# Two of the four channel chunks of a 31-tap depthwise convolution move from vector operations to matrix products with diagonal tap matrices

## The chip, the cores and the metric

One core of a Trainium2 chip runs the whole network. The metric is the device time of one execution in microseconds, the median of several runs. TensorE is called PE below, VectorE DVE, ScalarE ACT, GpSimd POOL and SyncE, which only starts transfers here, SP.

## The reference

The network has ten phases over 256 tokens with 1024 channels in float32: two blocks of a mixer and a convolutional feed-forward, then a second model whose first layer has the *even* mixer. Only that mixer is touched. Cut to what matters:

```python
def even_mixer(h, w_in, w_out, conv_w, conv_b, ln_g, ln_b, q_g, k_g, sinks):
    proj = h @ w_in                                  # 1024 -> 1792 columns
    a_val, a_gate, q, k, v = jnp.split(proj, cuts, axis=-1)
    u = a_val * jax.nn.sigmoid(a_gate)               # 512 channels
    u = lax.conv_general_dilated(u, conv_w[:, None, :], (1,), ((30, 0),),
                                 feature_group_count=512) + conv_b   # 31 taps, causal, per channel
    u = jax.nn.silu(layer_norm(u, ln_g, ln_b))
    q, k = rms_norm_2(q, q_g), rms_norm_2(k, k_g)    # 8 query heads, 2 key heads, 64 wide
    o, _, _ = banded_attention(q, k, v, 127, sinks)
    return jnp.concatenate([u, o], axis=-1) @ w_out
```

## The kernel before, in words

Activations lie transposed: 128 channels of a chunk on the partitions, the 256 tokens in a row. A weight matrix comes in *units* of 128 output columns (512 KB). For each unit SP loads `raw` (a ring of four slots), ACT copies it to a rounded high part `wh` (L507), DVE subtracts to get the low part `wl` (L761), and PE multiplies high by high, high by low and low by high (`tiles`, L1153 to L1155: 24 products of 128 by 128 with 256 tokens) into one of four PSUM banks `gb`. DVE scales the bank into the chunk `y` (L1041). SP's load of unit u+4 waits for DVE's split of unit u, and PE's unit u waits for the chunk that used its bank before.

The even mixer has 14 units on the way in and 8 on the way out. Chunks 0 to 7 of `y` are value and gate of the four channel chunks, chunk 8 is v, 9 is k, 10 to 13 are q. Every engine runs in its own order, and the order of the mixer's own work is one hand-written table `W["even"]` of entries (step, what, number): after unit `step` each engine does its share of the entries of this step, in the order of the table. So one entry places work on several engines at once. The entries that matter are

- `sig` g: ACT turns gate chunk g into its sigmoid, in place (L632).
- `conv` g: DVE does a quarter of the convolution of channel chunk g // 4 (`convolve`, L851 to L869). The first quarter multiplies value and gate into the padded operand `qqf` (L859), writes the first two taps into two accumulators (L861, L862) and adds six taps; the next ones add 8, 8 and 7 taps with one instruction each (L865), and the last adds the two accumulators (L869). There are 16 such entries, the last four between the heads of the attention.
- `turn`: PE transposes v (L1311). `sqr`, `sum`, `norm` g: the norm of q and k for group g (chunks 9 and 10, 11 and 12, 13): POOL squares (L427), PE sums over the head (L1298), ACT takes ln and then exp, each with a table load (L595, L597), DVE multiplies (L818).
- `attn` t: a software pipeline over 8 heads. PE turns the probabilities of head t-3 (L1265), makes the scores of head t (L1254) and the output of head t-4 (L1289); DVE takes the maximum of head t (L911 to L919) and normalises head t-1 (L932 to L946); ACT copies, and exponentiates head t (L544). Every second output DVE writes a low part into `mx` (L977).
- `ln`: the layer norm of the convolved chunks, and the gate (`layer_norm`, L871 to L899, with two PE sums), then the 8 units on the way out (L1166 to L1170).

```python
val, gate = yc(2 * c), yc(2 * c + 1)
for k in range(max(2, 8 * part), min(31, 8 * part + 8)):
    s = (val, gate)[k % 2]
    link_second(nc.vector.scalar_tensor_tensor(out=s, in0=qqf[:, k:k + SEQ], scalar=prm[:, taps + k:taps + k + 1],
                                               in1=s, op0=ALU.mult, op1=ALU.add))
```

Of the kernel before, what the change touches and what calls it, by code (L numbers as in the profile page):

```python
# [11 lines left out]
P = 128  # L12
# [86 lines left out]
def build_program(nc, xin, wa, wb, prm_d, row_d, const_d, bias_d, mask_d, pw_d, out):  # L99
# [21 lines left out]
    with ctx:  # L121
# [37 lines left out]
        qq = sb("qq", [P, 2, 2, SEQ])  # L159
        kk = sb("kk", [P, 2, 2, SEQ])  # L160
# [15 lines left out]
        low = ptb[:, :, :].rearrange("p a (b c) -> p a b c", b=2)  # L176
        ident = con[:, C_ID:C_ID + P]
# [31 lines left out]
        def cross_blocks(b):  # L209
# [16 lines left out]
        NAMES = ("qk_squared qk_sums qk_log qk_rsd qk_normed rotated roped v_transposed v_tokens scores maxima exps "  # L226
                 "probs probs_turned probsT attn_out attn_copied mix_psum mix_sbuf mix_hi mix_lo").split()
        OWN = {"mix1": ("gate_sigs gates_ready k_packed level_scores diag_copied level_copied totals q_up k_up stats "
                        "stats_log stats_rsd c_copied").split(),
               "even": "sigmoids ln_operand ln_sum ln_log ln_rsd ln_out ln_sig".split(), "odd": ["pooled"]}  # L230
# [36 lines left out]
        def row0(hs, t):  # L267
# [17 lines left out]
             "even": [(1, "sig", 0), (2, "conv", 0), (3, "sig", 1), (3, "conv", 1), (4, "conv", 2), (5, "sig", 2), (5, "conv", 3),  # L285
                      (6, "conv", 4), (7, "sig", 3), (7, "conv", 5), (8, "conv", 6), (9, "turn", 0), (9, "conv", 7),
                      (10, "conv", 8), (11, "sqr", 0), (11, "conv", 9), (12, "sum", 0), (12, "norm", 0), (12, "sqr", 1),
                      (12, "conv", 10), (13, "attn", 0), (13, "sum", 1), (13, "norm", 1), (13, "sqr", 2), (13, "conv", 11),
                      (14, "attn", 1), (14, "sum", 2), (14, "norm", 2), (14, "attn", 2), (14, "conv", 12), (14, "attn", 3),
                      (14, "attn", 4), (14, "conv", 13), (14, "attn", 5), (14, "attn", 6), (14, "conv", 14), (14, "attn", 7),  # L290
                      (14, "attn", 8), (14, "conv", 15), (14, "attn", 9), (14, "attn", 10), (14, "attn", 11), (14, "ln", 0)],
# [26 lines left out]
        def bank_of(kind, u):  # L318

            return u % 4 if kind != "mix1" or u < 13 else u % 2  # L320

# [179 lines left out]
        def _(act):  # L501
# [88 lines left out]
            def do(what, g, m, n, kind, l):  # L590
# [39 lines left out]
                elif what == "sig":  # L630
                    act.wait_ge(s_y, Y0[n] + 2 * g + 2)
                    nc.scalar.activation(yc(2 * g + 1), yc(2 * g + 1), ACT.Sigmoid).then_inc(m["sigmoids"], 1)  # L632
                elif what == "ln":
# [109 lines left out]
        def _(dve):  # L743
# [126 lines left out]

            def layer_norm(m):  # L871

                link(nc.vector.tensor_tensor(acc[:, :], yc(0), yc(2), ALU.add))
# [139 lines left out]
            def do(what, g, m, n, kind, l):  # L1013
# [4 lines left out]
                elif what == "gates":  # L1018
                    gates(m, l)
                elif what == "conv":  # L1020
                    convolve(m, g // 4, g % 4)
                elif what == "attn":
                    attention(m, kind, heads(kind), g, l)
                elif what == "level" and 1 <= g <= NL:
                    level(m, g)
                elif what == "post":
                    out_norms(m, l)
                elif what == "ln":
                    layer_norm(m)
                elif what == "pool":  # L1030
                    dve.wait_ge(m["mix_hi"], before(kind, "pool", g) + 1)
                    nc.vector.scalar_tensor_tensor(out=mc(ml, 4 + g), in0=MISC[:, 0:SEQ], scalar=col("ps", g),
                                                   in1=mc(mh, 4 + g).bitcast(f32), op0=ALU.mult, op1=ALU.subtract).then_inc(m["mix_lo"], 1)
# [111 lines left out]
        def _(pe):  # L1145
# [147 lines left out]
            def do(what, g, m, n, kind, l):  # L1293
# [42 lines left out]
                elif what == "post":  # L1336
                    pe.wait_ge(m["mix_sbuf"], 1)
                    pe.wait_ge(s_y, Y0[n] + IN_UNITS[kind])
                    for k, (c, w) in enumerate([(3, 2), (5, 2), (7, 1)]):
# [5 lines left out]
                        last.then_inc(m["mix_psum"], 1)  # L1345
                elif what == "ln":
# [188 lines left out]
```

## Time and profile before

| | us |
|---|---|
| median of 3 runs | 1840.45 |
| the three runs | 1834.74, 1840.45, 1840.59 |
| the profiled execution, its own time | 1835.33 |
| its span | 1833.6 |
| busy in the span: PE, DVE, ACT, POOL | 1673.1, 1273.2, 988.9, 531.1 |
| the even mixer's way in, attention and layer norm (974.6 to 1116.6 us of the span) | 142.0 |

The 1.7 us between the span and the profiled execution's own time lie around the span. Busy times of a stage come from a table of stretches; the granted clock there is a share of full speed, 1.00 being 2.4 GHz and 0.50 being 1.2 GHz. A matmul in f32 appears as two records in the trace, so x4 stands for two products. In a timeline the start of the next row tells more than the duration, since instructions of one engine overlap a little at their ends.

### The profile page before, as it was taken

The numbers are of one execution on the slowest core, as the hardware profiler recorded it, in microseconds if no ns is written. First come the engines' busy times: TensorE is split into PE (matmuls) and PEld (weight loads), VectorE is DVE, ScalarE is ACT, GpSimd is POOL, SyncE is SP. The second block draws the span as 40 slices with busy tenths as digits, with TensorE's granted clock in tenths as the row PEclk, the third lists the DMA queues.
The fourth block names the chain that finished last, engine by engine and source line by source line (L and its number), as shares of the span: only waits on it lengthen the run. The fifth ranks groups of instructions, "written<-read, shape, count | busy, mean of one in ns | idle before, by whom it ended". The sixth has DMA issues, their size and how long they took to land. (4 is left out here: it accounts for less than half of the span.)

```text
span 1833.6 us, 30207 instructions
## 1 busy us (share of the span) xinstructions
PE 1673.1 (91%) x10188; PEld 1448.8 (79%) x10188; DVE 1273.2 (69%) x2018; ACT 988.9 (54%) x1530; POOL 531.1 (29%) x511
## 2 busy tenths in 40 slices
PE   5896899999976999999999476999999999799999
PEld 5785799888856999888888335888888888568888
DVE  5675677756776777667757877777577765757763
ACT  5455466545563666466644344665376535446652
POOL 3040433310312334134410003443144411434430
PEclk9998899999997999999999658999999999789999
DMA  6330355654311456555654202556555654225563
GB/s 229 104 116 24 100 181 185 219 169 139 104 58 57 163 185 204 184 177 188 209 186 133 86 1 86 178 185 215 164 181 185 209 180 149 69 92 184 186 217 102
DMA packets 70793, 274.12 MB, mean 150 GB/s; under 512 B 7872, under 2 KB 9024, under 8 KB 70592
## 3 DMA queue, kind: packets, MB, share of 16 engines
q1 hardware_dynamic: 70272, 271.04, 45.9%
q0 software_dynamic: 448, 2.13, 0.3%
q8 instruction: 43, 0.70, 0.2%
q14 instruction: 30, 0.25, 0.0%
HBM read 272.09 MB, written 1.05 MB: 149 GB/s over the span
## 5 line engine op out<-in xcount | busy, mean ns | idle before, releaser
L761 DVE TENSOR_TENSOR wl<-raw,wh 128x1024 fp32r<-128x1024 f32 (+1 forms) x474 | 626.6, 1322 | 104.7 <-ACT wh L507 98.1
L507 ACT ACTIVATE wh<-raw 128x1024 fp32r<-128x1024 f32 (+1 forms) x474 | 529.2, 1118 | 211.9 <-PE gb L1170 125.2
L1166 PE MATMUL gb<-hx,wh 128*128 128x512 f32 x1540 | 554.0, 399 | 0.0
L1167 PE MATMUL gb<-hx,wl 128*128 128x256 f32 x1540 | 432.3, 281 | 0.0
L1166 PE MATMUL gb<-gux,wh 128*128 128x512 f32 x960 | 341.1, 394 | 0.0
L1166 PEld LDWEIGHTS gb<-hx,wh 128*128 128x128 f32 x1540 | 289.8, 188 | 60.7
L1153 PE MATMUL gb<-hx,wh 128*128 128x256 f32 x1008 | 299.2, 297 | 24.8 <-DVE wl L761 17.4
L1167 PEld LDWEIGHTS gb<-hx,wl 128*128 128x128 f32 x1540 | 291.0, 189 | 7.9
L1154 PE MATMUL gb<-hx,wh 128*128 128x256 f32 x1008 | 288.7, 286 | 0.0
L1155 PE MATMUL gb<-hx,wl 128*128 128x256 f32 x1008 | 288.2, 286 | 0.0
L1167 PE MATMUL gb<-gux,wl 128*128 128x256 f32 x960 | 268.1, 279 | 0.0
L493 POOL TENSOR_TENSOR tap<-tap,rstd 128x256 f32<-128x256 f32 x132 | 175.0, 1326 | 250.9 <-ACT tap L685 141.7
L1153 PEld LDWEIGHTS gb<-hx,wh 128*128 128x128 f32 x1008 | 196.0, 194 | 37.7 <-DVE wl L761 17.0
L1166 PEld LDWEIGHTS gb<-gux,wh 128*128 128x128 f32 x960 | 180.0, 188 | 39.1
L1154 PEld LDWEIGHTS gb<-hx,wh 128*128 128x128 f32 x1008 | 196.2, 195 | 5.2 <-issue 2.9
L496 POOL TENSOR_TENSOR gux<-gu,gux 128x256 f32 x132 | 142.8, 1082 | 197.5 <-ACT gux L694 197.5
L1155 PEld LDWEIGHTS gb<-hx,wl 128*128 128x128 f32 x1008 | 196.0, 194 | 0.0
L1167 PEld LDWEIGHTS gb<-gux,wl 128*128 128x128 f32 x960 | 180.4, 188 | 4.3
L413 POOL TENSOR_TENSOR sq<-x 128x256 f32<-128x256 f32 x70 | 70.0, 1000 | 241.7 <-DVE x L1114 222.2
L524 ACT ACTIVATE hx<-x,prm 128x256 fp32r<-128x256 f32 (+1 forms) x80 | 40.0, 508 | 145.4 <-DVE x L1114 142.9
L1166 PE MATMUL gb<-mx,wh 128*128 128x512 f32 x224 | 86.5, 422 | 12.6 <-DVE mx L899 9.1
L691 ACT ACTIVATE ptb<-gb 128x256 f32<-128x256 f32 x132 | 49.7, 377 | 81.5 <-PE gb L1170 81.5
(213 smaller groups left out, 2140.7 us busy)
## 6 DMA issues: line engine op xcount, KB each, us to landing
raw<-in_wa SPq DMA_DIRECT2D x378, 512.0 KB, 3.5
raw<-in_wb SPq DMA_DIRECT2D x96, 704.0 KB, 4.1
x<-in_x SPq DMA_DIRECT2D x1, 1024.0 KB, 5.0
out_x<-x SPq DMA_DIRECT2D x8, 128.0 KB, 3.2
row<-in_row POOLq DMA_DIRECT2D x1, 836.0 KB, 10.6
tab<-in_bias SPq DMA_DIRECT2D x3, 256.0 KB, 4.6
con<-in_const POOLq DMA_DIRECT2D x1, 544.0 KB, 7.7
tab<-in_bias SPq DMA_DIRECT2D x1, 512.0 KB, 5.2
```

Source lines behind the costliest of these rows:

```text
L413: link(nc.gpsimd.tensor_tensor(sq[:, 0:SEQ], xc, xc, ALU.mult))
L493: nc.gpsimd.tensor_tensor(tap[:, j, :], tap[:, j, :], rstd[:, :], ALU.mult).then_inc(s_up, 1)
L496: nc.gpsimd.tensor_tensor(gul[:, part], gu[:, j, :], guh[:, part].bitcast(f32), ALU.subtract).then_inc(s_gul, 1)
L507: nc.scalar.activation(wh[:, slot, 0:nt * P], raw[:, slot, 0:nt * P], ACT.Copy).then_inc(s_hi, 1)
L524: nc.scalar.activation(hh[:, part], x[:, part], ACT.Copy, scale=prm[:, at0]).then_inc(s_hh, 1)
L691: nc.scalar.activation(low[:, j, 1, :], gb[2 * j + 1][:, SEQ:2 * SEQ], ACT.Copy).then_inc(s_vl, 1)
L761: nc.vector.tensor_tensor(wl[:, slot, 0:nt * P], raw[:, slot, 0:nt * P], wh[:, slot, 0:nt * P].bitcast(f32), ALU.subtract).then_inc(s_lo, 1)
L1153: nc.tensor.matmul(bank, a, rhs_h(k), start=start and k == 0, stop=False)
L1154: nc.tensor.matmul(bank, a, rhs_l(k), start=False, stop=False)
L1155: last = nc.tensor.matmul(bank, b, rhs_h(k), start=False, stop=stop and k == nt - 1)
L1166: nc.tensor.matmul(bank[:, :], a, both(k), start=start and k == 0, stop=False)
L1167: nc.tensor.matmul(bank[:, 0:SEQ], b, high(k), start=False, stop=False)
```

## The change

The channel chunks 0 and 2 stay on DVE (`conv` 0 to 3 and 8 to 11). The chunks 1 and 3 are convolved on PE:

- `operand` (DVE): multiplies value and gate of the chunk into a padded buffer in free chunks of `y`.
- `diag` g (ACT): writes 8 (or 7) diagonal matrices, the identity times the tap of each channel, into a new buffer `dg` of 31 matrices; 62 copies of 128x128 in all. The second chunk's reuse the buffer behind the first's products.
- `taps` g (PE): 8 (or 7) products of a diagonal matrix with the shifted operand, in full f32, summed in PSUM bank `gb[3]`; 62 in all.
- `convolved` (ACT): copies the bank out with the bias.

So the units on the way in have three banks instead of four (`u % 3`). The layer norm waits for both `convolved`. The ln and exp instructions of the norms are as before. Semaphores that a phase doesn't use are no longer made for it.

```diff
+        with ExitStack() as turn:
+            dg = sb("dg", [P, 31, P], f32, turn)
...
+        operand = (y[:, 15 * SEQ:17 * SEQ], y[:, 17 * SEQ:19 * SEQ])
...
-             "even": [(1, "sig", 0), (2, "conv", 0), (3, "sig", 1), (3, "conv", 1), (4, "conv", 2), (5, "sig", 2), (5, "conv", 3),
...
+             "even": [(1, "sig", 0), (1, "diag", 0), (2, "conv", 0), (2, "diag", 1), (3, "sig", 1), (3, "operand", 0),
+                      (3, "conv", 1), (3, "diag", 2), (4, "conv", 2), (4, "diag", 3), (5, "sig", 2), (5, "taps", 0),
+                      (5, "conv", 3), (6, "taps", 1), (6, "conv", 8), (7, "sig", 3), (7, "taps", 2), (7, "operand", 1),
+                      (7, "conv", 9), (8, "taps", 3), (8, "conv", 10), (8, "diag", 4), (9, "turn", 0), (9, "convolved", 0),
+                      (9, "conv", 11), (9, "diag", 5), (10, "diag", 6), (11, "sqr", 0), (11, "diag", 7), (12, "sum", 0),
+                      (12, "norm", 0), (12, "sqr", 1), (12, "taps", 4), (13, "attn", 0), (13, "sum", 1), (13, "norm", 1),
+                      (13, "sqr", 2), (13, "taps", 5), (14, "attn", 1), (14, "sum", 2), (14, "norm", 2), (14, "attn", 2),
+                      (14, "taps", 6), (14, "attn", 3), (14, "attn", 4), (14, "taps", 7), (14, "attn", 5),
+                      (14, "convolved", 1)] + [(14, "attn", t) for t in range(6, 12)] + [(14, "ln", 0)],
...
         def bank_of(kind, u):
 
+            if kind == "even":
+                return u % 3
             return u % 4 if kind != "mix1" or u < 13 else u % 2
...
+                elif what == "diag":
+                    if g >= 4:
+                        act.wait_ge(m["taps_multiplied"], g - 3)
+                    for k in taps_of(g % 4):
+                        last = nc.scalar.activation(dg[:, k, :], ident, ACT.Copy, scale=col("ecw", 31 * (2 * (g // 4) + 1) + k))
+                    last.then_inc(m["diagonals"], 1)
+                elif what == "convolved":
+                    c = 2 * g + 1
+                    act.wait_ge(m["taps_multiplied"], 4 * g + 4)
+                    nc.scalar.activation(yc(2 * c), gb[3][:, 0:SEQ], ACT.Identity, bias=col("ecb", c)).then_inc(m["convolved"], 1)
...
+                dve.wait_ge(m["sigmoids"], c + 1)
+                nc.vector.memset(operand[g][:, 0:30], 0.0)
+                nc.vector.tensor_tensor(operand[g][:, 30:30 + SEQ], yc(2 * c), yc(2 * c + 1), ALU.mult).then_inc(m["operands"], 1)
...
+                elif what == "taps":
+                    c = g // 4
+                    pe.wait_ge(m["operands"], c + 1)
+                    pe.wait_ge(m["diagonals"], g + 1)
+                    if g == 4:
+                        pe.wait_ge(m["convolved"], 1)
+                    for k in taps_of(g % 4):
+                        last = nc.tensor.matmul(gb[3][:, 0:SEQ], dg[:, k, :], operand[c][:, k:k + SEQ], start=k == 0, stop=k == 30)
+                    last.then_inc(m["taps_multiplied"], 1)
```

The order of ACT at the start of the mixer, before (L632 is the sigmoid, L507 the split of a unit):

```order
L530 ACTIVATE rstd<-rstd 128x256
L507 ACTIVATE wh<-raw 128x1024 x2
L632 ACT_TABLE_LOAD
L632 ACTIVATE y<-y 128x256
L507 ACTIVATE wh<-raw 128x1024 x2
```

and with the change (L643 is the sigmoid, L518 the split, L648 a diagonal matrix):

```order
L541 ACTIVATE rstd<-rstd 128x256
L518 ACTIVATE wh<-raw 128x1024 x2
L643 ACT_TABLE_LOAD
L643 ACTIVATE y<-y 128x256
L648 ACTIVATE dg<-con,prm 128x128 x8
L518 ACTIVATE wh<-raw 128x1024
L648 ACTIVATE dg<-con,prm 128x128 x8
L518 ACTIVATE wh<-raw 128x1024
```

Eight diagonal matrices now stand ahead of the split of unit 6, and eight more ahead of that of unit 7.

The order of PE behind the last unit of the way in, before (L1254 scores, L1298 sums of squares, L1265 turned probabilities, L1289 outputs):

```order
L1155 MATMUL gb<-hx,wl 128x256
L1254 MATMUL mb<-y 128x256 x2
L1298 MATMUL mb<-sq,con 128x512
L1254 MATMUL mb<-y 128x256 x2
L1298 MATMUL mb<-sq,con 128x256
L1254 MATMUL mb<-y 128x256 x2
L1265 MATMUL mb<-con,pr 128x128 x4
L1254 MATMUL mb<-y 128x256 x2
L1265 MATMUL mb<-con,pr 128x128 x4
L1254 MATMUL mb<-y 128x256 x2
L1289 MATMUL mb<-ptb,tv 64x256 x2
L1265 MATMUL mb<-con,pr 128x128 x4
```

and with the change (the same work on L1285, L1329, L1296 and L1320; L1384 the taps):

```order
L1186 MATMUL gb<-hx,wl 128x256
L1285 MATMUL mb<-y 128x256 x2
L1329 MATMUL mb<-sq,con 128x512
L1384 MATMUL gb<-y,dg 128x256 x8
L1285 MATMUL mb<-y 128x256 x2
L1329 MATMUL mb<-sq,con 128x256
L1285 MATMUL mb<-y 128x256 x2
L1384 MATMUL gb<-y,dg 128x256 x8
L1296 MATMUL mb<-con,pr 128x128 x4
L1285 MATMUL mb<-y 128x256 x2
L1296 MATMUL mb<-con,pr 128x128 x4
L1285 MATMUL mb<-y 128x256 x2
```

Taps stand ahead of the scores of head 1, of the first turned probabilities and, three rows further on, of the third. The first four entries of taps stand behind the units 5, 6, 7 and 8, the fifth behind unit 12.

## Rows read from the trace of the kernel before

**Rows 1.** Stretches: us, busy PE, PEld, DVE, ACT, POOL, PEclk, DMA share, GB/s
```profile
986.50:1043.00 56.50, 37.66 (x256) 33.87 (x255) 55.19 (x117) 16.63 (x19) 3.10 (x2) 0.85 0.34 111
1043.00:1062.00 19.00, 5.63 (x14) 2.96 (x14) 8.98 (x24) 10.26 (x20) 0.72 (x1) 0.50 0.08 28
1062.00:1100.00 38.00, 29.65 (x80) 15.52 (x78) 31.11 (x90) 14.27 (x49) 0.00 (x0) 0.54 0.00 1
```

**Rows 2.** Timeline of DVE, first chunk: start us, us, engine line op, [idle before]
```profile
985.34 1.23 DVE L761 TENSOR_TENSOR wl<-raw,wh 128x1024 fp32r<-128x1024 f32 x1 [0.60 <-ACT wh L507]
986.52 0.39 DVE L859 TENSOR_TENSOR qq<-y 128x256 f32<-128x256 f32 x1
...
990.21 0.43 DVE L1041 TENSOR_TENSOR y<-gb,rstd 128x256 f32<-128x256 f32 x1
...
991.68 3.25 DVE L865 SCALAR_TENSOR_TENSOR y<-qq,prm,y 128x256 f32<-128x256 f32 x8
...
1004.73 0.43 DVE L1041 TENSOR_TENSOR y<-gb,rstd 128x256 f32<-128x256 f32 x1
```

**Rows 3.** Timeline of PE: one unit of the projection, and the longest wait
```profile
974.63 0.28 PE L1153 MATMUL gb<-hx,wh 128*128 128x256 f32 x1
...
977.51 0.63 PE L1177 MATMUL mb<-acc,con 128*128 128x256 f32 x2
...
1015.22 0.69 PE L1311 MATMUL mb<-con,y 128*128 128x128 f32 x2 [10.57 <-DVE y L1041]
```

**Rows 4.** Timeline of ACT: eight short instructions in a row
```profile
8.13 3.30 ACT L524 ACTIVATE hx<-x,prm 128x256 fp32r<-128x256 f32 x8
```

**Rows 5.** Groups by line and shape on ACT: busy us, mean ns of one
```profile
L632 ACT ACTIVATE y<-y 128x256 f32<-128x256 f32 x4 | 1.7, 419 | 17.1 <-DVE y L1041 17.1
L639 ACT ACTIVATE y<-y 128x1024 f32<-128x1024 f32 x1 | 1.1, 1057 | 1.6 <-DVE y L891 1.6
```

**Rows 6.** Timeline of PE: f32 products at the full clock (first two rows) and half
```profile
77.86 1.13 PE L1254 MATMUL mb<-y 64*128 64x256 f32 x4
78.92 1.08 PE L1289 MATMUL mb<-ptb,tv 128*64 128x256 f32 x4
...
1052.29 1.22 PE L1298 MATMUL mb<-sq,con 128*128 128x256 f32 x2 [8.52 <-POOL sq L427]
...
1083.67 1.12 PE L1265 MATMUL mb<-con,pr 128*128 128x128 f32 x4
1084.71 2.07 PE L1254 MATMUL mb<-y 64*128 64x256 f32 x4
1086.71 1.97 PE L1289 MATMUL mb<-ptb,tv 128*64 128x256 f32 x4
```

**Rows 7.** Timeline of DVE from the last projected chunk to the last attention output
```profile
1041.68 0.43 DVE L1041 TENSOR_TENSOR y<-gb,rstd 128x256 f32<-128x256 f32 x1
...
1050.49 0.88 DVE L818 SCALAR_TENSOR_TENSOR y<-y,prm,sq 128x256 f32<-128x256 f32 x2 [5.47 <-ACT sq L597]
...
1055.06 0.69 DVE L911 SCALAR_TENSOR_TENSOR pr<-tab,mb 128x512 f32<-128x512 f32 x1
...
1061.98 0.48 DVE L818 SCALAR_TENSOR_TENSOR y<-y,prm,sq 128x256 f32<-128x256 f32 x1 [4.13 <-ACT sq L597]
...
1099.89 0.42 DVE L977 TENSOR_TENSOR mx<-mb,mx 128x256 fp32r<-128x256 f32 x1 [2.15 <-ACT mx L587]
```

**Rows 8.** Granted clock (PEclk) in short stretches; columns as in Rows 1
```profile
1004.70:1008.40 3.70, 0.00 (x0) 0.00 (x0) 3.60 (x8) 0.00 (x0) 0.00 (x0) 1.00 0.25 66
1008.40:1015.20 6.80, 0.00 (x0) 0.00 (x0) 6.62 (x16) 2.31 (x3) 0.00 (x0) 0.51 0.36 120
1081.80:1089.70 7.90, 7.90 (x20) 4.05 (x20) 7.49 (x22) 2.07 (x8) 0.00 (x0) 0.50 0.00 0
1091.90:1096.80 4.90, 4.89 (x13) 2.27 (x14) 3.94 (x11) 0.60 (x1) 0.00 (x0) 0.50 0.00 0
1096.80:1099.40 2.60, 2.33 (x12) 1.39 (x12) 0.42 (x1) 0.98 (x2) 0.00 (x0) 0.91 0.03 6
```

More of the change, by code:

```diff
@@ L224, in build_program @@
         s_eps, s_ini, s_inie = sem("eps_set"), sem("start_values"), sem("start_exps")
-        NAMES = ("qk_squared qk_sums qk_log qk_rsd qk_normed rotated roped v_transposed v_tokens scores maxima exps "
-                 "probs probs_turned probsT attn_out attn_copied mix_psum mix_sbuf mix_hi mix_lo").split()
-        OWN = {"mix1": ("gate_sigs gates_ready k_packed level_scores diag_copied level_copied totals q_up k_up stats "
+        NAMES = ("qk_squared qk_sums qk_log qk_rsd qk_normed v_transposed v_tokens scores maxima exps "
+                 "probs probs_turned probsT attn_out mix_hi mix_lo").split()
+        OWN = {"mix1": ("rotated roped attn_copied mix_psum mix_sbuf gate_sigs gates_ready k_packed level_scores diag_copied level_copied totals q_up k_up stats "
                         "stats_log stats_rsd c_copied").split(),
-               "even": "sigmoids ln_operand ln_sum ln_log ln_rsd ln_out ln_sig".split(), "odd": ["pooled"]}
+               "even": "mix_sbuf sigmoids diagonals operands taps_multiplied convolved ln_operand ln_sum ln_log ln_rsd ln_out ln_sig".split(), "odd": ["mix_psum", "pooled"]}
         M = {n: {w: sem(f"{k}{l}_{w}") for w in NAMES + OWN[k]}
@@ L284, in build_program @@
                      [(26, "attn", t) for t in range(8, 14)] + [(26, "post", 0)],
-             "even": [(1, "sig", 0), (2, "conv", 0), (3, "sig", 1), (3, "conv", 1), (4, "conv", 2), (5, "sig", 2), (5, "conv", 3),
[L286 to L291, printed above, removed]
+             "even": [(1, "sig", 0), (1, "diag", 0), (2, "conv", 0), (2, "diag", 1), (3, "sig", 1), (3, "operand", 0),
[7 more added lines that the diff above has]
+                      (14, "convolved", 1)] + [(14, "attn", t) for t in range(6, 12)] + [(14, "ln", 0)],
              "odd": [(2, "turn", 0), (4, "turn", 1), (5, "sqr", 0), (6, "sum", 0), (6, "norm", 0), (7, "sqr", 1), (8, "sum", 1),
@@ L318, in bank_of, with taps_of @@
         def bank_of(kind, u):
+            if kind == "even":
+                return u % 3
             return u % 4 if kind != "mix1" or u < 13 else u % 2
+        def taps_of(part):
+            return range(8 * part, min(31, 8 * part + 8))
         def freed_by(kind, u):
@@ L869, in convolve, with operand_of @@
                     link(nc.vector.tensor_tensor(val, val, gate, ALU.add))
+            def operand_of(m, g):
+                c = 2 * g + 1
+                dve.wait_ge(m["sigmoids"], c + 1)
+                nc.vector.memset(operand[g][:, 0:30], 0.0)
+                nc.vector.tensor_tensor(operand[g][:, 30:30 + SEQ], yc(2 * c), yc(2 * c + 1), ALU.mult).then_inc(m["operands"], 1)
             def layer_norm(m):
+                dve.wait_ge(m["convolved"], 2)
                 link(nc.vector.tensor_tensor(acc[:, :], yc(0), yc(2), ALU.add))
@@ L1021, in do @@
                     convolve(m, g // 4, g % 4)
+                elif what == "operand":
+                    operand_of(m, g)
                 elif what == "attn":
```

## The prediction

> **What bounds the kernel now.** I read first the busy time by stage of the even mixer, then DVE's timeline, since DVE is nearly full, then PE's, then the granted clock. From 986.5 to 1043 us, the way in, DVE is busy 55.19 of 56.50 us and PE 37.66 [rows 1]: DVE sets the pace. In the hole behind it (1043 to 1062) nobody is full, DVE 8.98 us: the norms of q and k go round POOL, PE, ACT and DVE. In the attention (1062 to 1100) DVE has 31.11 us of 38 and PE 29.65 at a granted clock of 0.54, so both are near. The convolution is on the path: from L859 to the third next chunk is 1004.73 - 986.52 = 18.21 us, and less three pairs of L1041 and L761 (991.68 - 990.21 = 1.47 us each) that is 13.8 us for one channel chunk [rows 2]. PE shows the other side: it sat idle 10.57 us for a chunk that DVE had not scaled yet [rows 3].
>
> **What goes and what comes.** Two chunks leave DVE: 2 x 13.8 = 27.6 us. Two operands come: a product like L859 and a small memset, some 0.4 us each. POOL and SP get nothing new.
>
> **A tap on PE.** No row shows a chain of full 128x128 f32 products. Nearest is the pair of scores, x4 records for two products with other weights each: 78.92 - 77.86 = 1.06 us, so 0.53 us for 256 columns at the full clock [rows 6]. At half the clock the same pair took 1086.71 - 1084.71 = 2.00 us, so 1.00 us a product [rows 6]. I take 0.53 where the clock is full and 1.00 where it is half: 8 taps are 4.2 or 8.0 us, all 62 are 33 or 62 us.
>
> The Trainium skill, page "FP8 and Floating Point Precision", section "TensorE Precision Notes", says that true f32 takes four passes through the array. If that were all, a tap would be an estimated 4 x 256 / 2.4 GHz = 0.43 us and the taps together 6 us cheaper than by the row; I go by the row, which is dearer.
>
> **A diagonal matrix on ACT.** Eight copies of 256 columns with a scale per channel took 3.30 us, 0.51 of it the last one alone, so 0.40 us each in a row [rows 4]. A column costs (1057 - 419) / 768 = 0.83 ns [rows 5], so 128 columns fewer is 0.11 less: 0.29 to 0.30 us, 2.4 us for eight, 18 us in all. The bounds are 0.2 and 0.4 us. ACT was busy 16.63 of 56.50 us [rows 1], so most of it lies beside other work. Not all: the first eight stand ahead of the split of unit 6, for which DVE already waited 0.60 us [rows 2]. So that split, and the convolution behind it, come 2.4 us later.
>
> **The way in.** PE must now carry 14 units, the taps 0 to 4 and the small products. Its first taps wait for the operand of chunk 1, which stands on DVE behind the delayed split (987.7 to 988.9), the first quarter (990.21 - 986.52 = 3.7 us), one L1041 and one L761: ready near 994.7, taps from 995. Before that PE idles some 3 us. From there PE has 31 taps of 0.53 (16.4), the units 6 to 13, of 977.51 - 974.63 = 2.88 us each [rows 3] (23.0), the turned v (0.35), the sum of squares (1.0) and eight more taps (4.2): 45.0 us, to 1040. DVE needs less by then, since only eight quarters are left on it. So the last chunk is scaled at 1040.1 where it was 1041.68 [rows 7]: **-1.6 us**. Four quarters fewer on DVE give almost nothing here, because PE takes over as the bound. That is also why three banks instead of four cost nothing: DVE scales a chunk long before PE comes back to its bank.
>
> **The hole.** From the last chunk to L818 of group 1 it was 8.8 us. I add 0.8: ACT's last split is now released by PE's last unit. That L818 then comes at 1049.7. Behind it a quarter and its wait, 1055.06 - 1050.49 less the 0.8 us of L818 itself, 3.8 us, are gone [rows 7], so the maximum of head 1 starts at 1050.5 instead of 1055.06, and the norm of group 2 6.9 us later, at 1057.4 instead of 1061.98: **-4.6 us** in all so far. PE's part is eight taps between the sum and the scores of head 1, 1042.2 to 1046.4, done in time. Then PE waits for POOL's square, which came 1.8 us behind L818 [rows 6, 7]: idle from 1047.4 to 1051.5, 4.1 us.
>
> **The attention.** From 1061.98 to 1099.89 it was 37.9 us, 13.8 of them chunk 3's quarters between the heads. Without them 24.1 remain. But the last two sets of taps, 4.2 + 3.7 = 7.9 us at the full clock, now stand on PE ahead of the turned probabilities of heads 0 and 2. At worst none of it hides: 24.1 + 7.9 = 32.0 us, to 1089.4, which is 10.5 us earlier than now. What follows (layer norm, way out) is unchanged.
>
> **The clock decides what is left of that.** In the kernel before the clock held at 1.00 for the 3.7 us after PE ran dry at 1004.7 and then fell to about half (0.51) [rows 8]. PE's new wait of 4.1 us at 1047.4 is a little longer, so I expect a fall near 1051.5. Going up is less sure: PE was busy all of the 7.90 us from 1081.8 and stayed at 0.50, but after 4.90 busy us from 1091.9 it had 0.91 [rows 8]. The taps are the densest f32 work that PE has here, so I take it that the clock comes back about 5 us into them. That costs the sum (0.5), the scores (1.0) and three or four taps at 0.47 us more each: 3 us. The last heads have waits between them and will probably see half the clock again, 4 outputs or turns more expensive by about a half us each: 2 us. So -10.5 + 5 = -5.5; with the taps partly hidden behind DVE's maxima I say **-6 us**.
>
> The sum is made against the profiled execution, 1835.33 us: 1829.3. The median is 1840.45, 5 us above it, though one run was at 1834.74; the prediction is for the median: **1834 us**. Both kernels' runs can tell a difference of about 0.3%, 5.5 us here.
>
> **The rivals.**
>
> (a) *PE keeps its clock.* The taps close the gaps on PE so well that it stays at 1.00, or loses it for a moment only. For it: from 995 to 1047 PE has no gap. Against: the 4.1 us hole, and the small waits between heads. It gives -9 to -12 us, 1830. The Trainium skill, page "TensorE: Matmul & The Clock Gate", section "Why this matters for your kernels", says to keep TensorE busy without gaps and it stays at the full clock; by that rule every set of taps would lift it, which the 7.90 us at 0.50 above contradict.
>
> (b) *PE at half the clock becomes the bound of the attention, and the kernel is slower.* If the fall at 1051.5 is not undone, PE's queue from there is 1.0 (sum) + 6 x 2.0 (scores) + 8 x 1.04 (turned) + 8 x 1.97 (outputs) [rows 6] + 15 x 1.0 (taps) = 52 us, to 1103.5, and with two or three us of waits to 1106: **+6 us**, 1846. For it: the stage had 0.54 in the mean before [rows 1]. Against: taps fill the array, which half-height scores don't. If the clock is lost even before the taps behind unit 12, 15 more f32 products cost 0.47 us more each: +12, 1852. It decides at about one thing: whether the clock in the sixth and seventh set of taps is nearer 0.5 than 1. The break-even is near, since eight and seven taps and the heads between them at half clock undo some 6 of 10 us.
>
> (c) *Nothing to measure.* The clock comes back late, after the seventh set began: -3 to +1, 1839.
>
> (d) *The taps are not as priced.* At 0.43 or at 0.6 us the way in moves by 39 x 0.1 = 4 us either way.
>
> **How the numbers follow.** The forecast (the clock falls once in the hole and is back within the sixth set) 0.34; (a) 0.24; (c) 0.18; (b) 0.24, (d) being spread over them. The range leaves out the last tenth on each side: low end -11 against the faster base (1835.33), 1825; high end +8.5 against the median, 1849. Faster by more than 0.3%: all of (a) and two thirds of the forecast, 0.46. Within 0.3%: the rest of the forecast, (c) and a bit of (b), 0.32. Slower: 0.22.
>
> **What would show it.** DVE: two groups fewer of L865's kind, 58 instead of 116, and the way in no longer full. PE: busy without a wait from 995 to 1040 and 62 f32 products of 0.53 us; the last chunk scaled near 1040, the first norms' L818 near 1050, the last output's low part near 1094. ACT: 62 copies at 0.30 us in a row, and the split of unit 6 at 987. I am wrong if the taps run at another price, if the last chunk comes later than 1043 (then PE or ACT delays the way in more than I count), or if the granted clock in the attention is as low as before.

## The result, and the profile after

| | before | changed |
|---|---|---|
| median, first comparison (6 runs each) | 1840.38 us | 1818.94 us |
| lowest and highest | 1834.74, 1840.64 | 1815.19, 1830.52 |
| the profiled execution, its own time | 1835.33 us | 1816.97 us |

The ratio is 0.9905, 95% interval 0.9884 to 0.9926: faster by 17.5 us (14 to 21). I had predicted 1834 us and a range of 1825 to 1849, so the time lies below the range. The medians of this comparison are 21.4 us apart. Two later comparisons of the same kernel gave medians of 1821.13 against 1835.84 and 1821.25 against 1834.46, 14.7 and 13.2 us apart.

A total is a blunt tool here: in the profiles of all kernels of this study the start of the second phase, up to which nothing differs, lay anywhere between 218.0 and 229.2 us. So below I use **the mixer's own stretch**, from the start of its first norm's ln on ACT to that of the next phase's first norm (978.52 to 1146.03 before, 976.97 to 1127.80 in the change). It was 167.5 us before and 150.8 with the change, 16.7 less, and 150.9 in both later profiles of the change. Times "from the mark" count from the first of these two.

The page of the change, the lines of busy time and of the granted clock (before, PEclk had a 6, a 5 and an 8 where 9, 8, 8 now stand; DVE had 1273.2 us, PE 1673.1, ACT 988.9):

```profile
PE 1682.8 (93%) x10312; PEld 1463.1 (81%) x10312; DVE 1246.6 (69%) x1956; ACT 1007.7 (56%) x1594; POOL 530.6 (29%) x511
PEclk9998899999997999999999988999999999789999
```

Stretches of the change, same columns as [rows 1]: the way in, the hole, the attention.

```profile
985.00:1043.00 58.00, 55.75 (x350) 50.06 (x349) 47.95 (x100) 36.30 (x84) 2.99 (x2) 0.97 0.35 117
1043.00:1053.40 10.40, 6.07 (x13) 4.05 (x14) 3.45 (x11) 7.50 (x13) 0.61 (x1) 0.57 0.00 0
1053.40:1082.00 28.60, 23.37 (x109) 15.11 (x107) 17.97 (x56) 14.64 (x50) 0.00 (x0) 0.98 0.00 1
```

Before, DVE was busy 55.19 of 56.50 us on the way in and PE 37.66; now PE has 55.75 of 58.00. The attention took 37.9 us at a granted clock of 0.54 and now takes 28.6 at 0.98.

DVE of the change (answers to [rows 7]; L782 is the split of a unit, L1072 the scaling of a chunk, L839 the norm, L940 the maximum of a head, L1006 the low part of an output):

```profile
986.13 1.23 DVE L782 TENSOR_TENSOR wl<-raw,wh 128x1024 fp32r<-128x1024 f32 x1 [2.94 <-ACT wh L518]
...
1036.01 0.42 DVE L1072 TENSOR_TENSOR y<-gb,rstd 128x256 f32<-128x256 f32 x1
...
1045.64 0.88 DVE L839 SCALAR_TENSOR_TENSOR y<-y,prm,sq 128x256 f32<-128x256 f32 x2 [5.47 <-ACT sq L608]
1046.43 0.68 DVE L940 SCALAR_TENSOR_TENSOR pr<-tab,mb 128x512 f32<-128x512 f32 x1
...
1053.35 0.48 DVE L839 SCALAR_TENSOR_TENSOR y<-y,prm,sq 128x256 f32<-128x256 f32 x1 [4.13 <-ACT sq L608]
...
1082.00 0.42 DVE L1006 TENSOR_TENSOR mx<-mb,mx 128x256 fp32r<-128x256 f32 x1 [1.99 <-ACT mx L598]
```

From the marks, the last chunk came at 59.0 us (before 63.2), the norm of group 2 at 76.4 (83.5) and the last low part at 105.0 (121.4). So 4.1 us came from the way in, 3.0 from the hole (7.1 so far) and 9.3 from the attention; 0.3 came behind it.

PE of the change, taps are L1384:

```profile
992.96 5.41 PE L1384 MATMUL gb<-y,dg 128*128 128x256 f32 x16 [1.98 <-DVE y L897]
998.02 0.47 PE L1184 MATMUL gb<-hx,wh 128*128 128x256 f32 x1
...
1001.07 3.62 PE L1384 MATMUL gb<-y,dg 128*128 128x256 f32 x16
1004.34 0.47 PE L1184 MATMUL gb<-hx,wh 128*128 128x256 f32 x1
...
1038.19 3.62 PE L1384 MATMUL gb<-y,dg 128*128 128x256 f32 x16
1041.74 1.13 PE L1285 MATMUL mb<-y 64*128 64x256 f32 x4
1047.33 1.22 PE L1329 MATMUL mb<-sq,con 128*128 128x256 f32 x2 [4.46 <-POOL sq L438]
1048.48 2.07 PE L1285 MATMUL mb<-y 64*128 64x256 f32 x4
1050.48 5.83 PE L1384 MATMUL gb<-y,dg 128*128 128x256 f32 x16
1056.15 0.60 PE L1296 MATMUL mb<-con,pr 128*128 128x128 f32 x4
```

A set of eight taps took 1004.34 - 1001.07 = 3.27 us, 0.41 us a tap, where I had taken 0.53. The first set took 5.06 us and the seventh 5.67. The stretches (columns as above) say why: PE was at half the clock in both.

```profile
991.00:993.00 2.00, 0.04 (x1) 0.04 (x1) 2.00 (x5) 1.54 (x6) 0.00 (x0) 1.00 0.00 0
993.00:997.00 4.00, 4.00 (x11) 3.23 (x12) 3.91 (x10) 4.00 (x13) 0.00 (x0) 0.57 0.38 135
997.00:1005.00 8.00, 8.00 (x52) 7.41 (x51) 7.91 (x18) 2.52 (x4) 0.00 (x0) 1.00 0.36 117
1042.90:1047.30 4.40, 0.00 (x0) 0.00 (x0) 1.63 (x4) 2.66 (x4) 0.61 (x1) 0.69 0.00 0
1047.30:1053.00 5.70, 5.67 (x12) 3.74 (x13) 1.77 (x7) 4.61 (x10) 0.00 (x0) 0.50 0.00 0
1053.00:1055.00 2.00, 2.00 (x6) 1.60 (x6) 1.61 (x3) 0.32 (x1) 0.00 (x0) 0.55 0.00 0
1055.00:1083.00 28.00, 21.77 (x105) 13.81 (x103) 17.37 (x57) 15.64 (x50) 0.00 (x0) 1.00 0.00 1
...
1044.00:1044.50 0.50, 0.00 (x0) 0.00 (x0) 0.00 (x0) 0.50 (x1) 0.00 (x0) 1.00 0.00 0
1044.50:1045.00 0.50, 0.00 (x0) 0.00 (x0) 0.00 (x0) 0.49 (x2) 0.00 (x0) 0.55 0.00 0
```

The clock fell twice, once behind the 1.98 us wait for the first operand (which I had not forecast) and once in the hole (which I had). In the hole it held for only 1.7 us after PE ran dry at 1042.87 (the last two rows). From 1055 us to the last output it stayed at 1.00.

The groups by line, from 978 to 1100 us (count | busy us, mean ns | idle before):

```profile
L1384 PE MATMUL gb<-y,dg 128*128 128x256 f32 x124 | 32.2, 418 | 2.0 <-DVE y L897 2.0
L886 DVE SCALAR_TENSOR_TENSOR y<-qq,prm,y 128x256 f32<-128x256 f32 x58 | 23.6, 478 | 0.1
L648 ACT ACTIVATE dg<-con,prm 128x128 f32<-128x128 f32 x62 | 18.9, 389 | 0.0
```

As forecast, 58 scaled additions are left. The diagonal matrices took 0.29 us each in a row (eight from 986.00 to 988.35), for a forecast of 0.29 to 0.30.

### The profile page after: what moved, and what is told of

Same layout as the page of the kernel before. It is cut to its first block and busy times, and to the rows that moved or that the text cites. A ratio compares the mean times of both kernels' runs of the same rounds, so it can differ in the third digit from the quotient of the medians.

```text
span 1815.1 us, 30456 instructions
## 1 busy us (share of the span) xinstructions
PE 1682.8 (93%) x10312; PEld 1463.1 (81%) x10312; DVE 1246.6 (69%) x1956; ACT 1007.7 (56%) x1594; POOL 530.6 (29%) x511
## 5 line engine op out<-in xcount | busy, mean ns | idle before, releaser
L782 DVE TENSOR_TENSOR wl<-raw,wh 128x1024 fp32r<-128x1024 f32 (+1 forms) x474 | 627.4, 1324 | 108.7 <-ACT wh L518 102.5
L518 ACT ACTIVATE wh<-raw 128x1024 fp32r<-128x1024 f32 (+1 forms) x474 | 529.2, 1118 | 209.0 <-PE gb L1201 124.8
L1184 PEld LDWEIGHTS gb<-hx,wh 128*128 128x128 f32 x1008 | 193.7, 192 | 37.3 <-DVE wl L782 17.5
L507 POOL TENSOR_TENSOR gux<-gu,gux 128x256 f32 x132 | 142.6, 1081 | 197.4 <-ACT gux L715 197.4
```

The source lines that it names most:

```text
L507: nc.gpsimd.tensor_tensor(gul[:, part], gu[:, j, :], guh[:, part].bitcast(f32), ALU.subtract).then_inc(s_gul, 1)
L518: nc.scalar.activation(wh[:, slot, 0:nt * P], raw[:, slot, 0:nt * P], ACT.Copy).then_inc(s_hi, 1)
L782: nc.vector.tensor_tensor(wl[:, slot, 0:nt * P], raw[:, slot, 0:nt * P], wh[:, slot, 0:nt * P].bitcast(f32), ALU.subtract).then_inc(s_lo, 1)
L1184: nc.tensor.matmul(bank, a, rhs_h(k), start=start and k == 0, stop=False)
```

## The experiments

**The parts of the change apart (e1, e2).** e1 makes all the additions and takes nothing from DVE: the `conv` entries of all four chunks stay, and the result from PE goes to an unused chunk.

```diff
-                    nc.scalar.activation(yc(2 * c), gb[3][:, 0:SEQ], ACT.Identity, bias=col("ecb", c)).then_inc(m["convolved"], 1)
+                    nc.scalar.activation(yc(20 + g), gb[3][:, 0:SEQ], ACT.Identity, bias=col("ecb", c)).then_inc(m["convolved"], 1)
```

> The additions of the change without its removal: ACT builds the 62 diagonal matrices, PE makes the 62 products (their result goes to a free chunk that nothing reads), three banks, and DVE still convolves all four chunks. Theory A (the gain is DVE's work taken away, PE's idle time pays for the taps): no gain, 1838 to 1845 us, and DVE is full on the way in as before. Theory B (the gain is the granted clock that the taps keep up in the attention): at least a third of the 21 us comes with the additions alone, 1833 us or less, with the clock from the last projected chunk to the last attention output near 0.9 instead of 0.54.

Measured: 1840.44 us, ratio to the kernel before 1.0014 (0.9992 to 1.0035); the mixer's stretch 170.8 us, 3.3 more than before. From the norm of group 2 to the last low part (columns as above):

```profile
1065.14:1103.24 38.10, 26.23 (x94) 15.45 (x94) 31.02 (x89) 14.63 (x50) 0.00 (x0) 0.82 0.00 1
```

This is 38.1 us at a granted clock of 0.82 where it was 37.9 at 0.53. The higher clock alone is worth nothing while DVE has 31.0 us to do there. Theory A holds: no gain by the additions alone.

e2 keeps the structure and takes the load off: of each set only the first tap and its matrix remain, so the chunks 1 and 3 lack 54 of their 62 taps.

```diff
-                    for k in taps_of(g % 4):
+                    for k in taps_of(g % 4)[:1]:
```

> The removal without most of the additions: chunks 1 and 3 get 8 products and 8 diagonal matrices (the first of each set) instead of 62, so their convolution is left out but for those taps. Theory A: PE has 54 products of 0.41 us less, of which some 13 us lay on the way in, where PE was the bound, and up to 6 in the attention: 1803 to 1812 us. Theory B: PE falls to half clock in the attention without the taps and the gain over the change is small or none, 1816 us or more, with a granted clock near 0.54 there.

Measured: 1812.01 us, ratio 0.9870 (0.9841 to 0.9899); the mixer's stretch 147.8 us, 19.7 less than before and only 3.1 less than the change. The total lies at the upper edge of theory A's range (1803 to 1812). The two parts add up: +3.3 - 19.7 = -16.4 against -16.7. The last chunk came at 55.3 us from the mark, the norm of group 2 at 72.7, and then

```profile
1048.08:1077.67 29.59, 21.44 (x82) 12.16 (x80) 18.02 (x57) 14.66 (x50) 0.00 (x0) 0.80 0.00 1
```

So the attention without its taps took **longer** than with them (29.6 against 28.65 us): its clock was 0.80 against 0.97. The 0.9 us are lost before the first low part of an output (16.5 us behind the norm of group 2, for 15.5 with the change), and up to 1060 us, 11.9 us behind that norm, e2's clock was 0.50; behind that both kernels run alike. I had put this stretch at 24.1 us without taps.

**The hole filled (e3).** The seventh set goes into PE's idle 4.46 us.

```diff
-                      (13, "sqr", 2), (13, "taps", 5), (14, "attn", 1), (14, "sum", 2), (14, "norm", 2), (14, "attn", 2),
-                      (14, "taps", 6), (14, "attn", 3), (14, "attn", 4), (14, "taps", 7), (14, "attn", 5),
+                      (13, "sqr", 2), (13, "taps", 5), (14, "attn", 1), (14, "taps", 6), (14, "sum", 2), (14, "norm", 2), (14, "attn", 2),
+                      (14, "attn", 3), (14, "attn", 4), (14, "taps", 7), (14, "attn", 5),
```

> The seventh set of taps (8 products) moved one place ahead on PE, before the sum of group 2: into the 4.5 us in which PE waits for POOL's square and after which its clock fell to 0.50. Theory A with the clock: PE stays at 1.00 in the stretch, the set is off the path (it took 5.7 us there), 4 to 6 us faster than the change, 1813 to 1815 us, and the spread of the runs (15 us with the change) becomes smaller since the clock is no longer a draw. Rival: heads 0 to 2 wait for the norm of group 2 anyway, and it is within 1 us of the change.

Measured: 1824.65 us, ratio 0.9924 (0.9899 to 0.9949); the mixer's stretch 154.3 us, 3.5 **more** than the change, which neither theory had. The norm of group 2 stayed at 76.4 us. PE in the place after it:

```profile
1052.65 3.72 PE L1384 MATMUL gb<-y,dg 128*128 128x256 f32 x16
1057.16 0.70 PE L1329 MATMUL mb<-sq,con 128*128 128x256 f32 x2 [0.78 <-POOL sq L438]
...
1061.56 1.08 PE L1296 MATMUL mb<-con,pr 128*128 128x128 f32 x4 [2.65 <-ACT sq L606]
...
1067.57 1.09 PE L1296 MATMUL mb<-con,pr 128*128 128x128 f32 x4 [2.92 <-ACT ptb L585]
```

and the clock, then the whole attention:

```profile
1052.00:1060.00 8.00, 6.13 (x26) 4.21 (x24) 3.41 (x10) 5.21 (x11) 0.61 (x1) 1.00 0.00 0
1060.00:1063.00 3.00, 1.44 (x5) 1.14 (x6) 0.00 (x0) 2.96 (x4) 0.00 (x0) 0.72 0.00 0
1067.57:1076.82 9.25, 9.25 (x27) 6.20 (x28) 3.96 (x15) 3.41 (x13) 0.00 (x0) 0.60 0.00 0
```
```profile
1063.18:1095.30 32.12, 23.97 (x94) 14.47 (x92) 18.03 (x57) 14.65 (x50) 0.00 (x0) 0.82 0.00 1
```

The clock held through the hole, as expected, and fell one wait later, when the heads needed it. What that cost can be read from PE. The second turned probabilities (1067.57 above) start 4.4 us behind the norm of group 2 in the kernel before, in the change and in e3 alike. From there to the end of the eighth set PE has the same 27 records and no wait in both; e3 takes 9.25 us for them at 0.60, the change 5.78 at 1.00:

```profile
1057.74:1063.52 5.78, 5.78 (x27) 4.25 (x27) 5.14 (x16) 3.01 (x12) 0.00 (x0) 1.00 0.00 0
```

These 3.5 us are the whole loss. In the change the slow seventh set stands in just the waits ahead: it runs at half the clock while DVE and ACT make the norm and the first probabilities, it doesn't delay the second ones, and PE comes out of it at 1.00.

**Three banks (e4).** The kernel before, with the one line of the change that takes a bank away.

```diff
+            if kind == "even":
+                return u % 3
```

> The kernel before with three PSUM banks for the units of the even mixer instead of four, nothing else. My reading (DVE scales each chunk well before PE comes back to its bank): no change, 1839 to 1841 us. Rival: where DVE sets the pace, PE's unit now waits a DVE round longer: 2 to 5 us slower, 1842 to 1845 us, which the change then paid and got back elsewhere.

Measured: 1833.3 us against 1836.29 beside it, ratio 0.9987 (0.9971 to 1.0003); the mixer's stretch 167.6 against 167.5. Three banks cost nothing.

**The change again (e5, e12).** The same kernel, unchanged, to see how far its times repeat.

> The changed kernel as it is, beside the three below on one chip, since the first four had no run of it beside them. Both theories: 1815 to 1825 us, 18 to 22 us under the kernel before. The even mixer alone, from its first norm's ln to that of the next phase, 150.8 us in the first profile of it and 167.5 in that of the kernel before: 150 to 152 again. If that stretch moves by more than 2 us between two profiles of one kernel, differences of 3 us between profiles say nothing.

Measured: 1821.13 us, ratio 0.9914 (0.9891 to 0.9937), stretch 150.9. And later, beside e11:

> The changed kernel once more, beside e11 on one chip, for a direct comparison: even mixer 150.8 to 150.9 us as in both profiles of it so far, total 1816 to 1824.

Measured: 1821.25 us, ratio 0.9934 (0.9911 to 0.9956), stretch 150.9, the last low part at 105.0 us each time. So differences of half a microsecond between stretches can be read, where totals can't show them. (That rests on three profiles of one kernel; the kernels below have one each, and e9 and e10 ran on another chip than e5 and e12.)

**The matrices behind the splits (e6).**

```diff
-             "even": [(1, "sig", 0), (1, "diag", 0), (2, "conv", 0), (2, "diag", 1), (3, "sig", 1), (3, "operand", 0),
-                      (3, "conv", 1), (3, "diag", 2), (4, "conv", 2), (4, "diag", 3), (5, "sig", 2), (5, "taps", 0),
+             "even": [(1, "sig", 0), (2, "conv", 0), (2, "diag", 0), (3, "sig", 1), (3, "operand", 0), (3, "diag", 1),
+                      (3, "conv", 1), (4, "conv", 2), (4, "diag", 2), (4, "diag", 3), (5, "sig", 2), (5, "taps", 0),
```

> The eight diagonal matrices of the first set move behind the split of unit 6 on ACT, the second set behind that of unit 7, and so on. Theory A (from DVE's late start on, PE's queue is the bound of the way in): DVE's wait of 2.94 us for the split of unit 6 falls below 1 us, the operand and the first taps come 2 us earlier, and the way in and the whole are 2 us shorter: even mixer 148.8 us, total 2 us under the change. Rival B: the units' own supply bounds PE early on (PE waits for split or load of the units 4 and 5 in any case), the taps start earlier but the last chunk does not move: 0 us, even mixer 150.8.

Measured: 1820.77 us, ratio 0.9908 (0.9883 to 0.9933), against 0.9914 for the change beside it; stretch 150.5. The first set of taps, and the attention:

```profile
996.36 3.62 PE L1384 MATMUL gb<-y,dg 128*128 128x256 f32 x16
999.63 0.47 PE L1184 MATMUL gb<-hx,wh 128*128 128x256 f32 x1
```
```profile
1056.56:1086.77 30.21, 24.99 (x109) 15.63 (x107) 18.03 (x56) 14.65 (x50) 0.00 (x0) 0.94 0.00 1
```

Both theories are half right. As theory A has it, DVE's wait for the split fell to 0.60 us, the taps began without a wait and at full clock (3.27 us), the last chunk came at 56.7 us instead of 59.0 and the norm of group 2 at 74.0 instead of 76.4. But then 1.6 of the 2.4 us went again in the attention, where the clock fell among the last heads, and 0.4 behind it. Rival B's number came out, for another reason than B's.

**Every tap twice (e7).** The chunks 1 and 3 come out as twice their sum.

```diff
-                    for k in taps_of(g % 4):
+                    for i, k in enumerate([*taps_of(g % 4), *taps_of(g % 4)]):
```

> Every set of taps is issued twice in a row into the same sum, so the two chunks on PE come out doubled (all but the order of other work as in the change). Prices the taps. Theory A (0.41 us a tap; on the way in PE is the bound; the set in the hole is free): the 31 + 8 taps of the way in lengthen it by 39 x 0.41 = 16 us, the eight in the hole behind the norm of head 1's group cost nothing (3.3 us of a 4.5-us wait), the 15 in the attention 6.2 us less what the waits of the heads hide, 2 us: +20 us against the change, even mixer 171. Rival B (the row I priced by, 0.53 us, holds under load, some taps wait for weights): +26 us. Rival C (PE has slack on the way in, DVE bounds it still): the way in under +8 us, +12 us in all.

Measured: 1843.68 us, ratio 1.0039 (1.0020 to 1.0057), 22.6 us over e5; stretch 175.1, 24.2 over. The sixth set, now 16 taps:

```profile
1053.08 7.07 PE L1384 MATMUL gb<-y,dg 128*128 128x256 f32 x32
1060.08 1.13 PE L1285 MATMUL mb<-y 64*128 64x256 f32 x4
```

Sixteen took 7.00 us where the eight of the change took 3.55 (1041.74 - 1038.19): 0.43 us for each tap more. The last chunk came 16.7 us later (75.7 against 59.0), 39 x 0.43, so on the way in every tap of PE counts. The norm of group 2 came 16.7 later too: the set in the hole is free, as theory A has it. The attention took 36.5 us instead of 28.65, 7.8 more where A had 4; its clock had fallen to 0.93. The sum lies between A and B, A's price is right.

**Only one chunk (e8).** Chunk 3 stays on DVE, in its old places; the layer norm waits for one `convolved`.

```diff
-                      (13, "sqr", 2), (13, "taps", 5), (14, "attn", 1), (14, "sum", 2), (14, "norm", 2), (14, "attn", 2),
-                      (14, "taps", 6), (14, "attn", 3), (14, "attn", 4), (14, "taps", 7), (14, "attn", 5),
+                      (13, "sqr", 2), (14, "attn", 1), (14, "sum", 2), (14, "norm", 2), (14, "attn", 2), (14, "conv", 12),
+                      (14, "attn", 3), (14, "attn", 4), (14, "conv", 13), (14, "attn", 5), (14, "attn", 6),
```

> Only chunk 1 is convolved on PE (31 taps, 31 diagonal matrices); chunk 3 stays on DVE with its four quarters between the heads, in the places they have in the kernel before. Theory A (each chunk pays where it stood: the way in by what PE then needs, the attention by the quarters that leave it): the way in loses also the eight taps of the fifth set, so the last chunk is scaled 3.3 us earlier than in the change, but the quarters in the attention stay: even mixer about 160 us, or 157 if the norms of the hole have no quarter in their way; total 7 to 9 us above the change. Rival B (most of the change's gain comes from the clock that the taps restore, since the taps of sets 5 to 7 stand in the low-clock stretch): without those sets the clock stays at 0.5 through the attention and the kernel is no faster than before, 167 us.

Measured: 1825.14 us, ratio 0.9950 (0.9927 to 0.9973); stretch 157.8, 6.9 over the change. The last chunk came at 57.6 us, the norm of group 2 at 74.9, and the attention was

```profile
1053.00:1090.03 37.03, 27.14 (x80) 14.35 (x78) 31.03 (x89) 14.15 (x49) 0.00 (x0) 0.64 0.00 1
```

as long as before, within a microsecond. So chunk 1 gave all that came before the attention (8.6 us), and chunk 3 gives 8.4 us in the attention and costs 1.5 ahead of it. The last chunk came 1.5 us earlier than in the change, for A's 3.3, and the medians of this one comparison are only 4.0 us apart for A's 7 to 9; the rest is as A has it. B's premise held only in part (the clock was 0.64, not 0.5), and the gain did not hang on it.

**Towards a faster version (e9, e10, e11).** All start from e6. e9 moves the fifth set off the way in and the sixth into the hole, and keeps a set behind head 2:

```diff
-                      (12, "norm", 0), (12, "sqr", 1), (12, "taps", 4), (13, "attn", 0), (13, "sum", 1), (13, "norm", 1),
-                      (13, "sqr", 2), (13, "taps", 5), (14, "attn", 1), (14, "sum", 2), (14, "norm", 2), (14, "attn", 2),
+                      (12, "norm", 0), (12, "sqr", 1), (13, "attn", 0), (13, "sum", 1), (13, "norm", 1),
+                      (13, "sqr", 2), (13, "taps", 4), (14, "attn", 1), (14, "taps", 5), (14, "sum", 2), (14, "norm", 2), (14, "attn", 2),
```

> The table of e6 with the fifth set of taps moved from behind unit 12 to behind unit 13 (where the sixth stood), and the sixth into PE's idle time ahead of the sum of group 2; the seventh and eighth stay. Theory A (all reasons so far): PE's queue ahead of unit 13 is 3.3 us shorter, so its chunk is scaled 3 us earlier than in e6, until the norm of the first group (54.2 us behind the first norm's ln in e6) becomes the limit: the norm of group 2 about 72.2 instead of 74.0. The hole is filled, the clock holds there, and the seventh set, which still follows the scores of head 2, runs at the full clock (3.3 us instead of 5.7) and keeps PE dense, which e3 lacked: the last low part 99 to 101 instead of 104.2 (105.0 in the change), even mixer 146 to 147, total 4 us under e5. Rival B (the clock falls later instead, as in e3, when PE waits for ACT and DVE between heads): gain of the way in kept, that of the attention lost, even mixer 149 to 151. Rival C: the clock's late fall costs more than before, as in e3: 154.

e10 also puts the eighth set behind head 7, e11 cuts the last two sets in pieces between the heads (`taps_a` the first four, `taps_b` the rest):

```diff
-                      (14, "taps", 6), (14, "attn", 3), (14, "attn", 4), (14, "taps", 7), (14, "attn", 5),
+                      (14, "taps_a", 6), (14, "attn", 3), (14, "taps_b", 6), (14, "attn", 4), (14, "taps_a", 7), (14, "attn", 5),
+                      (14, "attn", 6), (14, "attn", 7), (14, "taps_b", 7), (14, "attn", 8), (14, "convolved", 1)] + [(14, "attn", t) for t in range(9, 12)]
```

> As e9, and the last set of taps moves from behind head 4's step to behind that of head 7, whose scores are the last ones, so that no scores stand behind it. Theory A: DVE's wait of 1.88 us for scores behind that set goes, and the set stands in PE's wait of 2.59 us for the last heads' probabilities: 1 us under e9. Rival B (the stretch of the heads 3 to 7 without taps lets the clock fall as in e3): scores, turned probabilities and outputs at half the clock, 2 to 3 us over e9.

> As e9, but the last two sets of taps are cut into pieces of four or three: behind the scores of head 2, behind the step of head 3 (which begins with the first turned probabilities), behind that of head 4 and behind that of head 7. In e9 PE waited 3.5 us for the first probabilities right behind a whole set, and its clock fell there, in e10 again at head 5. Theory A (pieces of 1.6 us in the gaps between heads keep PE from a wait long enough to lose the clock): the granted clock stays at 1.00 from the way in to the last head, last low part 99 to 100.5 us behind the first norm's ln (e9 104.0, e10 103.0, the change 105.0), even mixer 146 to 147.5. Rival B (the heads' own waits are too long whatever stands between them): the clock falls at some head and stays low for 4 to 6 us, last low part 102 to 104, even mixer 149 to 150.

Measured: e9 1822.75 us, 0.9919 (0.9895 to 0.9943), stretch 150.3; e10 1821.29, 0.9898 (0.9874 to 0.9923), stretch 149.8; e11 1820.52, 0.9927 (0.9903 to 0.9951), stretch 150.7. Their attention, one row each in this order:

```profile
1059.32:1091.02 31.70, 23.39 (x94) 13.63 (x93) 18.03 (x57) 14.65 (x50) 0.00 (x0) 0.89 0.00 1
```
```profile
1059.29:1089.94 30.65, 24.62 (x94) 14.55 (x93) 18.02 (x56) 14.65 (x50) 0.00 (x0) 0.83 0.00 1
```
```profile
1050.16:1082.54 32.38, 27.46 (x99) 16.81 (x98) 18.03 (x57) 14.77 (x50) 0.00 (x0) 0.79 0.00 1
```

In all three the norm of group 2 came at 72.3 us, as I had said (72.2) and 4.1 earlier than in the change, and the clock was 1.00 all the way to there. And in all three the attention gave back 2.0 to 3.7 of it, e10 least. The fall that rival B names came in each, but its price only in e9. e10 was forecast 2 to 3 us over e9 by B and 1 us under it by theory A, and was 0.6 us under it by the stretch. e11 was worse than B had it: stretch 150.7 for 149 to 150, last low part at 104.7 for 102 to 104. The first fall stands near the same place as in e3: PE runs out of work around the norm, here waits 3.51, 3.50 and 2.40 us for the probabilities of the second head, and soon behind that wait its products run at half the clock. In e9:

```profile
1063.72 0.63 PE L1296 MATMUL mb<-con,pr 128*128 128x128 f32 x4 [3.51 <-ACT ptb L585]
1064.28 1.47 PE L1285 MATMUL mb<-y 64*128 64x256 f32 x4
1065.67 1.97 PE L1320 MATMUL mb<-ptb,tv 128*64 128x256 f32 x4
```

None of them beats the change by more than the totals can tell; by the stretch e10 is 1.0 us shorter, on another chip.

## Why the prediction was wrong, step by step

The step that failed is the attention, forecast at 36.5 us and measured at 28.65; a smaller part was the price of a tap. The steps in their order:

**The bound of the way in**: right. DVE set the pace before, PE does now; from 992.96 to 1042.87 us it has no wait. But DVE is close behind. With 34 of its 39 taps gone (e2) the last chunk came only 3.7 us earlier, since PE then waited 7.3 us for a chunk that DVE had not scaled, and with the fifth set gone from there (e9) it came 1.7 us earlier than in e6.

**The tap**: wrong. I took 0.53 us from a pair of scores at the full clock [rows 6]; the taps took 0.41 to 0.44 (0.43 by the doubled sets). By the 0.43 that is 0.10 x 39 = 3.9 us for the 39 taps on PE's way. The Trainium skill, page "FP8 and Floating Point Precision", section "TensorE Precision Notes", counts four passes for true f32, from which I had worked out an estimate of 0.43 us: the trace agrees, and I had weighed it and gone by the row. The row was of one pair of products 64 rows high, and a pair says little about a chain of eight; why it costs more a product, no run shows.

**The matrices on ACT**: right (0.29 us each), and so was the delay of unit 6's split: DVE's wait grew from 0.60 to 2.94 us, 2.3 for a forecast of 2.4. What I missed is that PE's idle 2 us ahead of the first taps made it lose the clock; that set took 5.06 us instead of 3.27. The taps also began at 16.0 us from the mark for a forecast of 995 - 978.52 = 16.5. Together: -3.9 + 1.8 - 0.5 = -2.6, and that is what the way in came out shorter than the forecast (last chunk at 59.0 us from the mark for a forecast of 1040.1 - 978.52 = 61.6).

**Three banks**: right, nothing (e4).

**The hole**: right, -3.0 us to the norm of group 2, as forecast.

**The attention**: this step failed most. I had 24.1 + 7.9 = 32.0 us, then added 5 us for the clock and took half a microsecond off: 36.5. It was 28.65, 7.9 less. Against e2's 29.6 us without most taps, the terms come apart so:

- *The 7.9 us of taps were put down as lying bare: 8.8 too much.* With the taps the stretch took 0.9 us less than without, not 7.9 more. The seventh set ran in waits (e3), and the clock was 0.97 with them and 0.80 without. That the taps hold the clock up is my reading of e2, where the taps and most of ACT's copies went together.
- *The 5 us for the clock: none of it came.* Of these, 3.5 (the sum, the scores and the last heads) were counted against a base that never had the full clock: the 24.1 us were what was left of a stretch at 0.54 [rows 1], so the heads were already priced at half the clock, and so were the sum and the scores in the hole (0.50 [rows 1]). The other 1.5 were for taps that I had priced at the full clock; the seventh set did run 2.4 us longer (5.67 for 3.27), but in waits.
- *The 24.1 was too low, by 5.5.* Taking DVE's 13.8 us out of a stretch does not shorten it by as much once DVE is no longer the bound. In e2's row no engine is full (PE 21.44, DVE 18.02, ACT 14.66 of 29.59 us), so I read the rest as the heads' chain from one engine to the next. Part of the 29.6 is e2's own half clock: by its rows up to 3 us; no run has the heads without taps at the full clock.

With the half microsecond: -8.84 - 5 + 5.49 + 0.5 = -7.85.

**The clock**: half right. It fell in the hole, at 67.6 us from the mark for a forecast of 1051.5 - 978.52 = 73.0: I had let it hold through the wait by [rows 8], where it held for 3.7 us, and it held for 1.7. It came back within the seventh set, by 1055, some 4.5 us into its taps (forecast 5; where the prediction says "within the sixth set" it must mean `taps` 6, the seventh in order, since the sixth ends before the wait). The fall among the last heads (2 us) did not come in the change; it did in e6, where the same work started 2.4 us earlier against the mark.

**The rivals**: nearest was (a), PE keeps its clock, with 9 to 12 us; it came nearest in the attention but was 5 us short of the 16.7, and the clock did fall twice. (b), that PE at half clock becomes the bound, did not come: its premise, that the fall isn't undone, failed. (d), the price of the tap, came true with 3.9 us. Two slips in the sums change nothing: 6 + 15 x 0.47 in (b) is 13 and not 12, and 1835.33 - 11 is 1824.3 and not 1825. From the forecast of -6 to the -16.7 of the profiles it is -2.6 on the way in, -7.9 in the attention and -0.3 behind it.

## What to carry to other kernels

Before you charge a lost clock to a change, look at which clock the rows that you build on were taken at; a stretch at half the clock can only gain. When the engine that is the bound loses work, its busy time is not what you win: find the chain that remains (an experiment with the work taken out says it, here 29.6 us where subtraction said 24.1). And where the clock falls in PE's waits, work put into a wait can cost nothing (the seventh set here), and moving it to where it seems free can cost more than it saves (e3, 3.5 us) or most of it (e9, some 3 of 4.1 us).

## What the runs showed of the hardware

- The clock's worth depends on the bound. With DVE at 31.0 us in the attention, it took 37.9 us at 0.53, 37.0 at 0.64 and 38.1 at 0.82. With DVE at 18.0 it took 28.65 us at 0.97 (the change), 30.2 at 0.94 (e6), 29.6 at 0.80 (e2, hardly any taps), 31.7 at 0.89 (e9), 30.65 at 0.83 (e10), 32.1 at 0.82 (e3) and 32.4 at 0.79 (e11), though e3, e9 and e10 have about a set of taps less in that stretch than the change. The times are not in strict order of the clock; that it also counts which head the fall hits is my reading.
- A wait of 1.98 us at the full clock was followed by 3.4 us of half the clock in the change, while one of 1.91 us in e9 was followed by none. Closer still: in the change and in e6 PE does the same work with the same waits for some 16 us, up to a wait of 2.59 and 2.58 us for the last heads' probabilities. Behind it the clock stays in the change (first two rows) and falls in e6 (last two). Neither the length of the wait nor that work decides alone; what does, no run shows. So part of what a new order wins or loses here (e6's 1.6 us above all) need not come from that order itself, and I can't forecast it.

```profile
1076.49 1.05 PE L1320 MATMUL mb<-ptb,tv 128*64 128x256 f32 x4 [2.59 <-ACT ptb L585]
1077.47 0.66 PE L1296 MATMUL mb<-con,pr 128*128 128x128 f32 x4
```
```profile
1079.68 1.05 PE L1320 MATMUL mb<-ptb,tv 128*64 128x256 f32 x4 [2.58 <-ACT ptb L585]
1080.66 0.92 PE L1296 MATMUL mb<-con,pr 128*128 128x128 f32 x4
```

- The mixer's stretch repeats within 0.1 us from profile to profile (150.8, 150.9, 150.9), clock falls included, while the whole moves by some 10 us. What moves lies in the first phase, up to 229.2 us; why, I haven't tried.
